# Encoder kernel, blocks of seven products: order of the sixth and seventh exchanged

## What is computed

```python
def squared_relu_mlp(h, w_up, w_down):
    return jnp.square(jax.nn.relu(h @ w_up)) @ w_down
# per layer: x = x + rms_norm(squared_relu_mlp(rms_norm(x, g_pre), w_up, w_down), g_post)
```

## Time and profile before

| | |
|---|---|
| median of three runs | 1905.82 us |
| the profiled execution's own time | 1902.94 us |
| its span, first to last instruction | 1901.1 us |
| granted TensorE clock, mean | 0.997 of full speed |
| PE busy | 1854.4 us, 98% |
| DVE busy | 1160.8 us, 61% |
| ACT busy | 816.3 us, 43% |
| POOL busy | 382.8 us, 20% |

### The profile page before, as it was taken

The page is one execution under the profiler, slowest core; times in us unless marked ns, Lnnn a source line. Parts: engine busy times, 40 slices in busy tenths (PEclk is TensorE's granted clock), DMA queues, the critical chain, the costliest instruction groups (busy, mean ns, idle before and its releaser), DMA issues. The chain is left out here.

```text
span 1901.1 us, 28143 instructions
## 1 busy us (share of the span) xinstructions
PE 1854.4 (98%) x10762; PEld 1585.8 (83%) x10762; DVE 1160.8 (61%) x1647; ACT 816.3 (43%) x1433; POOL 382.8 (20%) x303
## 2 busy tenths in 40 slices
PE   9999999999999999999999999999999999999997
PEld 7785578889889888897889788897888898989897
DVE  6957956643787556766652356625474368847474
ACT  5216855434546253542123521225553355535362
POOL 0330006500022314103320033300200000522221
PEclk9999999999999999999999999999999999999999
DMA  4330014402233232322332022320351223232231
GB/s 166 121 100 23 1 49 146 150 12 89 79 93 108 89 110 81 119 74 83 98 105 75 31 92 89 99 68 34 134 177 56 67 68 111 78 111 93 95 109 48
DMA packets 99059, 167.73 MB, mean 88 GB/s; under 512 B 5632, under 2 KB 32384, under 8 KB 98688
## 3 DMA queue, kind: packets, MB, share of 16 engines
q1 hardware_dynamic: 98944, 166.15, 27.1%
HBM read 164.03 MB, written 2.10 MB: 87 GB/s over the span
## 5 line engine op out<-in xcount | busy, mean ns | idle before, releaser
L1245 DVE TENSOR_TENSOR w_lo<-raw,w_hi 128x1024 fp32r<-128x1024 f32 x256 | 332.6, 1322 | 255.9 <-ACT w_hi L738 254.4
L738 ACT ACTIVATE w_hi<-raw 128x1024 fp32r<-128x1024 f32 x256 | 264.6, 1057 | 355.4 <-PE ps L1919 344.1
L1919 PE MATMUL ps<-act_hi,w_lo 128*128 128x512 f32 x860 | 340.8, 396 | 6.9 <-DVE w_lo L1245 4.3
L1919 PE MATMUL ps<-act_lo,w_hi 128*128 128x512 f32 x864 | 336.4, 390 | 0.0
L1919 PE MATMUL ps<-act_hi,w_hi 128*128 128x512 f32 x860 | 335.6, 390 | 0.0
L1919 PEld LDWEIGHTS ps<-act_hi,w_lo 128*128 128x128 f32 x860 | 161.9, 188 | 45.2 <-DVE w_lo L1245 6.4
L1919 PEld LDWEIGHTS ps<-act_lo,w_hi 128*128 128x128 f32 x864 | 162.7, 188 | 35.0 <-issue 1.9
L1919 PEld LDWEIGHTS ps<-act_hi,w_hi 128*128 128x128 f32 x860 | 161.7, 188 | 34.1
L1919 PE MATMUL ps<-ff_lo,w_hi 128*128 128x512 f32 x448 | 177.0, 395 | 0.0
L1919 PE MATMUL ps<-ff_hi,w_hi 128*128 128x512 f32 x448 | 177.0, 395 | 0.0
L1919 PE MATMUL ps<-ff_hi,w_lo 128*128 128x512 f32 x448 | 177.0, 395 | 0.0
(11 more groups left out here) (252 smaller groups left out, 4030.2 us busy)
## 6 DMA issues: line engine op xcount, KB each, us to landing
raw<-in_db_w_qkv SPq DMA_DIRECT2D x72, 512.0 KB, 3.8
raw<-in_w_up SPq DMA_DIRECT2D x64, 512.0 KB, 3.7
raw<-in_w_down SPq DMA_DIRECT2D x64, 512.0 KB, 3.6
raw<-in_xa_wkv SPq DMA_DIRECT2D x32, 512.0 KB, 3.7
raw<-in_da_w_qkv SPq DMA_DIRECT2D x24, 512.0 KB, 3.9
raw<-in_xa_wq SPq DMA_DIRECT2D x16, 512.0 KB, 3.7
raw<-in_xa_wo SPq DMA_DIRECT2D x16, 512.0 KB, 3.7
raw<-in_da_w_o SPq DMA_DIRECT2D x8, 512.0 KB, 3.8
```

What stands on the lines that cost most here:

```text
L738: nc.scalar.activation(w_hi[:, g % 4], raw[:, g % 4], ACT.Copy).then_inc(w_hi_ready, 1)
L1245: nc.vector.tensor_tensor(w_lo[:, g % 4], raw[:, g % 4], w_hi[:, g % 4].bitcast(f32), ALU.subtract).then_inc(w_lo_ready, 1)
L1919: last = nc.tensor.matmul(ps[:, s + m, 0:width], left, right, start=(k == 0 and n == 0 and not early), stop=(k == KT - 1 and n == 2))
```

## The change

The last two product numbers are exchanged: T4 becomes the sixth (number 5) and A22 the seventh (number 6). Everything that goes by number moves with it: the slots, the order of ACT's rounding, of DVE's remainders and of PE's products. T4's weight is the lower right quarter w22 of `raw`, A22's is s4. PE's T4 waits for join 2, and A22 for join 3. The load of the odd slot is let go after six remainders (`P_T4 + 1`) instead of seven. POOL's line 672 is unchanged in its text (`P_A22 + 1`) and now stands for seven remainders instead of six. Join 4 stays behind the seventh product.

```diff
-P_A11, P_T2, P_T1, P_T3, P_A21, P_A22, P_T4 = range(PRODUCTS)
-BANK_OF = (0, 1, 2, 3, 0, 2, 3)
+P_A11, P_T2, P_T1, P_T3, P_A21, P_T4, P_A22 = range(PRODUCTS)
+BANK_OF = (0, 1, 2, 3, 0, 3, 2)
...
-            return (upper[:, :, 0:P], s2, s1, upper[:, :, P:2 * P], lower[:, :, 0:P], s4, lower[:, :, P:2 * P])[i]
+            return (upper[:, :, 0:P], s2, s1, upper[:, :, P:2 * P], lower[:, :, 0:P], lower[:, :, P:2 * P], s4)[i]
...
-                sp.wait_ge(mixed_lo, of_block(b, PRODUCTS, PRODUCTS if j % 2 else P_T3 + 1, ii))
+                sp.wait_ge(mixed_lo, of_block(b, PRODUCTS, (P_T4 if j % 2 else P_T3) + 1, ii))
...
-                    if i in (P_T2, P_T3, P_T4):
+                    if i in (P_T2, P_T3, P_A22):
...
-                    if i == P_T4:
+                    if i == P_A22:
...
+                        if i == P_T4:
+                            pe.wait_ge(product_joined, of_block(b, JOINS, 2, ii))
                         if i == P_A22:
                             pe.wait_ge(product_joined, of_block(b, JOINS, 3, ii))
```

## The result

The changed kernel took 1894.96 us (median of four runs, 1893.84 to 1896.93) against 1906.36 us of the kernel before in the same measurement: ratio 0.9944, 95% interval 0.9929 to 0.9959. A second measurement gave 1896.35 us (six runs) against 1905.93 us (24 runs), ratio 0.9948, interval 0.9935 to 0.9961. It is faster by about half a per cent, and both intervals exclude no change. Forecast were 1898.3 us within 1894.0 to 1903.2.

The account below looks back on a forecast made before the run. PE, 98% busy, was taken as bound by its work plus six pauses (11.2 us) at join 3, with DVE late. Gains of 0.54 and 0.73 us, taken as 1.25 x 6 = 7.5, gave 1905.8 - 7.5 = 1898.3 us, range 1894.0 to 1903.2.

Parts of the forecast that it names:

- holds: On DVE, a remainder that starts while a POOL sum runs ends 0.55 us after that sum, costing at most 1.1 us.
- Items 1 and 2: All 24 blocks: unchanged matmuls cost 0; PE's added wait per block costs 0, at most 2.9 us in all.
- Item 3: Third block of each run: T4 waits for join 2 instead of join 3 and starts 0.54 us earlier.
- Items 4 and 5: First block of a run: the odd slot's load goes earlier, so POOL's sums start 3.5 or 3.75 us earlier.
- Item 6: Block 12, DVE: 1.10 us of idle time absorbs a delay; the sixth remainder ends at 1641.23 instead of 1642.72.
- the walk: The prediction's step-by-step timing of DVE and POOL through blocks 12 to 14, giving T4 1.27 us earlier.
- Item 7: Second load: POOL starts at 1645.3 instead of 1647.36, and block 14's join 2 ends 0.73 us earlier, at 1656.84.
- Item 8: Block 14's T4 starts 1.27 us earlier, leaving a 0.44 us pause; 1.25 x 6 = 7.5 us in all.
- A: Third blocks: only PE's shorter wait counts, join 2 ends as now; gain 3.2 us, 1902.6 us, chance 0.12.
- B: Third blocks: the whole pause before the sixth product goes; gain 11.2 us, 1894.6 us, chance 0.07.
- C: Earlier POOL sums delay more DVE remainders; each run of four blocks loses 1.66 us, 1915.8 us, chance 0.04.
- D: Third blocks: nothing happens, as something else, such as T4's own remainder, is last; 1905.8 us, chance 0.03.

Follow-up runs that it names:

- the short sums: The kernel before with each of POOL's four sums cut to 128 of 512 columns: ratio 0.9937 to the kernel before, 1892.62 us at clock 0.997.
- the load as before: The changed kernel, but with the odd slot's load let go after seven remainders: ratio 0.9972 to the kernel before, 1901.07 us at clock 0.997.
- the sums late: The changed kernel with one more POOL wait, keeping its first sums at about their old time: ratio 0.9986 to the kernel before, 1902.92 us at clock 0.997.
- the load alone: The changed kernel, but with T4 waiting for join 3 instead of join 2: ratio 0.9979 to the kernel before, 1902.15 us at clock 0.997.

## Why the prediction was right, and where its sizes were off

- **What bounds** (11.2 us of pauses at join 3, caused by holds): shown, by the wait's going, by the short sums, and by ACT's having no wait for a sum in these stretches.
- **Items 1 and 2**, no cost of the matmuls and of the added wait: in the trace after, T4, which got the wait, follows at 0.12 us in the 14 blocks where join 2 is there in time, and A22 at 0.11 to 0.12 in all 24. 0 was right.
- **Item 3**, 0.54 us per run by PE's shorter wait: 0.53 to 0.55 in four runs of the kernel with it alone, nothing in two, where the race between sum and remainder went the other way. That is 2.2 us in that trace; by the times it was 3.3, and the item had 3.2. So the item's mechanism holds where no race turns, and its size for a typical execution stays open between the two.
- **Items 4 and 5**, the first set 3.5 to 3.75 us earlier: 2.30 us after the run's start instead of 5.72 in block 12, and 1.63 to 1.73 in the four runs where the seventh remainder releases it. Right.
- **Item 6**, the idle 1.10 us taking one hold, join 4 and the sixth remainder unheld: right, line by line, in block 12. The sixth remainder ended 11.23 us after the run's start, as the walk had it. In the other kind of run it was not: two remainders are held, the idle time pays for one, and T4 of the first block comes 0.03 to 0.12 us late. The prediction says that the same walk serves for both kinds, and there it was wrong.
- **Item 7** was off by 0.6 us at the second load. Its issue came 1.93 us behind that of the even slot (4.0 before), and it took 4.3 us to land instead of 3.7, so that POOL began at 15.93 and not 15.3. For that the remainder of 1641.79 was hardly held (0.74 us), which the walk had held to 1648.56, and a later one was held instead. The two nearly cancel: join 2 ended at 27.11, the walk had 26.84.
- **Item 8**, the sum: 7.5 us gained of 11.2 leaves 3.7 us of pauses, 2.95 measured; 7.8 us gained from the six runs of blocks, 8.1 at the same clock. Block 14 fell short (1.01 us gained of 1.27, 0.70 left instead of 0.44), and so did block 2; the four runs of the other kind gained 1.3 to 2.0 us where 1.2 to 1.3 were forecast, with the second set 1.6 to 2.3 us earlier (in the run of block 10 its holds on DVE fell from 4.2 us to 2.7). That the total came so near is in part luck: errors of both signs. What lies beyond 8.1 us in the medians fits the scatter of the clock in the second measurement; in the first it is 3.3 us, and no clocks are on record that would show it. The base that I took, the median of three runs, had the same scatter in it.
- **The rivals.** A is ruled out by the kernels with the load as before and with the sums late, which have 9.0 and 9.4 us of pauses against 3.0. B, no pause at all, came nearest in the time, 1894.6, but not in the mechanism: 2.95 us of pauses stayed. C has a trace in it. The prediction named pauses in a run's first or second block as its sign, and there are some, but far too small for its price: 0.03 to 0.12 us in four first blocks, where the earlier sums hold the remainder ahead of join 2; without the exchange they would be the 0.6 us that the load alone shows. D did not happen.

One thing the prediction did not see is that the parts need each other. It added 0.54 and 0.73 us per run; in the traces they bring 0.36 and 0.45 apart, for different reasons, and together 1.37.

## What to carry to other kernels

Where GpSimd and VectorE both work on SBUF operands, ask at what time GpSimd's instructions run, not only how long they take: put them beside VectorE's idle time or its PSUM reads, and what releases them (here a load let go by one count less) is the handle for that. Make each wait of TensorE ask for no more than the bank it writes, and in the stretch where VectorE is late put what TensorE waits for ahead of what only the next block needs. Differences of some tenths of a per cent are to be compared among runs at the same granted clock, or by pauses counted in the trace, and a race won or lost in one trace need not be typical of its kernel.

## What the runs showed of the hardware

- A VectorE subtraction of two SBUF operands that started 0.07 us after a GpSimd sum took 1.78 us, one that started 0.15 us ahead of it 0.69 us.
- The granted clock had a short drop to its lower level between 50 and 100 us in seven of the nine traces (means of the stretch 0.95 to 0.97 against 1.00), and between 900 and 1000 us in six (0.98), where PE was busy all the time; over the range of the runs' mean clock, 0.994 to 0.998, the kernel before took 1909.62 to 1902.12 us.
- A load of 512 KB issued 1.9 us behind another landed after 4.3 us; 4.0 us behind it, after 3.7. In the four traces with the earlier load, the eight second loads of the odd slot in a run that were issued 1.9 to 2.1 us behind landed after 4.2 to 4.7 us, the sixteen issued 2.4 to 3.1 us behind after 3.5 to 4.1.
